# Three operands of the top-k selection are read from PSUM banks instead of SBUF

## The chip, the core and the metric

The kernel runs on one core of a Trainium2 chip. Its five engines are TensorE (PE in the profile; its weight loads are PEld), VectorE (DVE), ScalarE (ACT), GpSimd (POOL) and SyncE (SP), which here only issues DMAs. The metric is the device time of one launch in microseconds (us); lower is better. The inputs lie in the chip's memory (HBM). SBUF and PSUM are the on-chip memories; PSUM has eight banks of 128 partitions x 512 float32 numbers, and it is what matmuls write.

## What is computed

Two blocks of a language model over 256 tokens of width 1024, in float32: retention and stick-breaking attention, then a mixture of 16,384 experts chosen by product keys ("peer"), then a gating mixer, a feed-forward layer, an RWKV-7 mixer and another feed-forward layer. The change lies in the choice of the experts:

```python
q = (xb @ w_q).reshape(B, T, 8, 2, 128)                 # 8 heads, two half queries
s1 = einsum('bthd,nd->bthn', q[..., 0, :], k1)          # 128 scores each
s2 = einsum('bthd,nd->bthn', q[..., 1, :], k2)
v1, i1 = lax.top_k(s1, 16)
v2, i2 = lax.top_k(s2, 16)
cand_s = (v1[..., :, None] + v2[..., None, :]).reshape(..., 256)
cand_i = (i1[..., :, None] * 128 + i2[..., None, :]).reshape(..., 256)
top_s, pos = lax.top_k(cand_s, 16)
idx = take_along_axis(cand_i, pos)
g = softmax(top_s)
h = einsum('bthkd,btd->bthk', u_tab[idx], xb)
a = gelu(h) * g
y = einsum('bthk,bthkd->btd', a, v_tab[idx])
```

## The kernel before, in words

The kernel gathers no rows of the two expert tables. It multiplies the tokens with all 128 tiles of 128 experts (`hidden`, one tile of `u` at a time), applies gelu, multiplies by a table of gates that is zero where an expert was not chosen, and multiplies the result with all tiles of `v`. So the choice of the experts is needed only for the gates, and runs on DVE while PE works through the first tiles of `u`.

**The tiles of `u`.** Each float32 tile is split in a high and a low part, so that three matmuls of a faster format give the product. For each tile ACT makes `rows_hi` from `rows_raw` (L1349), POOL subtracts, `rows_lo = rows_raw - rows_hi` (L2301: two inputs and one output of 1024 numbers a partition in SBUF), and PE runs 8 matmuls on `rows_hi` with `x_hi` and 8 with `x_lo` (L644, L645) and then, after a wait for `rows_lo`, 8 on `rows_lo` (L648). `rows_hi` has two buffers: ACT makes that of tile t + 2 when PE has finished tile t. ACT's gelu of a tile (L1334) reads one of PSUM banks 0 to 3 and writes the table. The rows come by DMA into a ring of eight, issued by SP as PE finishes tiles. The order on each engine is that of the code. Loops of eight tiles are called rounds.

**The selection on DVE**, once for each half `c` of 128 tokens, in the order of the code: `top16` on 16 lists of 128 scores (five passes over the lists: MAX8, FIND_INDEX8, MATCH_REPLACE8, MAX8, FIND_INDEX8); the indices turned into float32 (`top_if`, L1863); the 8 x 256 sums of candidates (`cand`, L1865); `top16` on these 8 lists; shifts and masks that split a position into its two halves (L1869, L1870), the margins for the softmax (L1873, which ACT's exponential at L1358 waits for), the positions as float32 (L1874); then, for j = 0 and 1, `oh` = (position == iota) (L1879), `oh` = `oh` * index (L1884), and a sum over the last axis into `pick` (L1887). L1865, L1879 and L1884 work on 2048 numbers a partition, with operands that are broadcast from 16 at a time.

Between these steps DVE waits for its own earlier ones (`step.sync`, or `step(...)`, which marks and waits). ACT takes the exponentials of both halves in one place, after its fifth round; DVE then scales `pick` and signals `pick_ready`; PE transposes `pick` after six rounds of tiles (L664), and DVE copies the results out (L1901) and makes one-hot rows (L1912), that turn into gates from the 65th tile on. PE fills banks 4 and 5 with the transposes and banks 6 and 7 with the gates; between the expert scores (`ps`, all eight banks) and the gates nobody uses banks 6 and 7.

Of the kernel before, what the change touches and what calls it, by code (L numbers as in the profile page):

```python
# [6 lines left out]
P = 128  # L7
# [3 lines left out]
TC = SEQ // P  # L11
HEADS = 8
# [3 lines left out]
TOPK = 16  # L16
SLOTS = HEADS * TOPK
# [14 lines left out]
ALU = mybir.AluOpType  # L32
# [86 lines left out]
def build(nc, d_x, d_const, d_param, d_rows, d_ring, d_k12, d_u, d_v, d_up, d_down, d_brow, d_final, d_out, upto=99):  # L119
# [3 lines left out]
    def S(name):  # L123
        if name not in sems:
            sems[name] = nc.alloc_semaphore(name)
        return sems[name]
# [5 lines left out]
    def view(name, at, shape, dt=F32):  # L132
        return nc.alloc_sbuf_tensor_at(name, [P] + list(shape), dt, offset=base + 4 * at)
# [39 lines left out]
    def C(name):  # L173
        a, w = CONST_AT[name]
        return const[:, a:a + w]
# [12 lines left out]
    a = ARENA_AT + TC * PROJ_W  # L188
# [20 lines left out]
    a = ARENA_AT  # L209
# [5 lines left out]
    cand = view("cand", a, [TC, HEADS, TOPK, TOPK])  # L215
# [1 line left out]
    top_v = view("top_v", a, [TC, 16, TOPK])  # L217
    a += 512
    top_i = view("top_i", a, [TC, 16, TOPK], U32)
    a += 512  # L220
    top_if = view("top_if", a, [TC, 16, TOPK])
    a += 512
    best = view("best", a, [TC, HEADS, TOPK])
    a += 256
# [140 lines left out]
    PS = [nc.alloc_psum_tensor(f"bank{b}", [P, 512], F32) for b in range(8)]  # L365
# [12 lines left out]
    def wait_filled(eng, name):  # L378
        b, _, fills = plan.at[name]
        eng.wait_ge(filled[b], fills)  # L380
        return PS[b]

    def wait_drained(eng, name):
        b, k, _ = plan.at[name]
        eng.wait_ge(drained[b], k + 1)
# [15 lines left out]
    def bc(ap, shape):  # L401
        return ap.to_broadcast([P] + list(shape))

    with nc.Block() as block:  # L404
# [3 lines left out]
        def _(pe):  # L408
# [11 lines left out]
            def release_when_filled(n, name):  # L420
                b, _, fills = plan.at[name]
                release[n] = (filled[b], fills)
# [1214 lines left out]
        def _(ve):  # L1637
            V = nc.vector
            step = Steps(ve, S("dve_steps"))
# [41 lines left out]
            def copy(name, dst):  # L1681
                o = wait_filled(ve, name)
                drain(name, V.tensor_copy(dst, o[:, :]))
# [152 lines left out]
            for b in range(0, 8, 2):  # L1836
                copy(("pq", b), qT[:, 2 * b:2 * b + 2, :].rearrange("p m t -> p (m t)"))

            def top16(n, src, val, idx):

                for m in range(n):
                    step.mark(V.max(val(m)[:, 0:8], src(m)))
                step.sync()
                for m in range(n):
                    step.mark(V.max_index(idx(m)[:, 0:8], val(m)[:, 0:8], src(m)))
                step.sync()
                for m in range(n):
                    step.mark(V.match_replace(src(m), val(m)[:, 0:8], src(m), KNOCKED_OUT))
                step.sync()
                for m in range(n):  # L1850
                    step.mark(V.max(val(m)[:, 8:16], src(m)))
                step.sync()
                for m in range(n):
                    step.mark(V.max_index(idx(m)[:, 8:16], val(m)[:, 8:16], src(m)))
                step.sync()

            for c in range(TC):
                for g in range(4):
                    wait_drained(ve, ("ps", c, g))
                top16(16, lambda m: sc[:, c, m, :], lambda m: top_v[:, c, m, :], lambda m: top_i[:, c, m, :])  # L1860
                if c:
                    step.sync()
                step.mark(V.tensor_copy(top_if[:, c, :, :], top_i[:, c, :, :]))  # L1863
                v4 = top_v[:, c, :, :].rearrange("p (h j) k -> p h j k", j=2)
                step(V.tensor_tensor(cand[:, c, :, :, :], bc(v4[:, :, 0, :].unsqueeze(3), [HEADS, TOPK, TOPK]),  # L1865
                                     bc(v4[:, :, 1, :].unsqueeze(2), [HEADS, TOPK, TOPK]), ALU.add))
                flat = lambda h: cand[:, c, h, :, :].rearrange("p a b -> p (a b)")
                top16(HEADS, flat, lambda h: best[:, c, h, :], lambda h: pos[:, c, h * TOPK:(h + 1) * TOPK])
                step.mark(V.tensor_scalar(pos12[:, 0, c, :], pos[:, c, :], 4, None, ALU.logical_shift_right))  # L1869
                step(V.tensor_scalar(pos12[:, 1, c, :], pos[:, c, :], TOPK - 1, None, ALU.bitwise_and))  # L1870

                g4 = pick[:, 2, c, :].rearrange("p (h k) -> p h k", h=HEADS)
                V.tensor_tensor(g4, best[:, c, :, :], bc(best[:, c, :, 0:1], [HEADS, TOPK]), ALU.subtract).then_inc(S("margin_ready"), 1)  # L1873
                step(V.tensor_copy(pos12f[:, :, c, :], pos12[:, :, c, :]))  # L1874
                i4 = top_if[:, c, :, :].rearrange("p (h j) k -> p h j k", j=2)

                wait_filled(ve, ("ps", TC - 1, 3))
                for j in range(2):
                    step.mark(V.tensor_tensor(oh[:, j, :, :], bc(pos12f[:, j, c, :].unsqueeze(2), [SLOTS, TOPK]),  # L1879
                                              bc(C("iota")[:, 0:TOPK].unsqueeze(1), [SLOTS, TOPK]), ALU.is_equal))  # L1880
                step.sync()
                for j in range(2):
                    o4 = oh[:, j, :, :].rearrange("p (h k) a -> p h k a", h=HEADS)
                    step.mark(V.tensor_tensor(o4, o4, bc(i4[:, :, j, :].unsqueeze(2), [HEADS, TOPK, TOPK]), ALU.mult))  # L1884
                step.sync()
                for j in range(2):
                    step.mark(V.tensor_reduce(pick[:, j, c, :], oh[:, j, :, :], AX, ALU.add))  # L1887
                step.sync()
# [107 lines left out]
            for b in range(4):  # L1996
                o = wait_filled(ve, ("sp", b))
                for m in range(2):
                    n = 2 * b + m
# [191 lines left out]
            c = NRC - 1  # L2191
# [51 lines left out]
            c = NRC - 1  # L2243
# [250 lines left out]
def _program(nc, arrays, upto=99):  # L2494
    aps = [nc.dram_tensor(f"in_{n}", a.shape, F32, kind="ExternalInput").ap() for n, a in arrays.items()]
    out = nc.dram_tensor("out_0", (SEQ, D), F32, kind="ExternalOutput").ap()
    build(nc, *aps, out, upto=upto)
# [11 lines left out]
```

## Time and profile before

| | |
|---|---|
| median of 3 runs | 1954.88 us (1953.95 to 1955.27) |
| the profiled execution, its own time | 1953.33 us |
| its span, first to last instruction | 1951.5 us |
| PE busy | 1799.9 us, 92% of the span |
| POOL, DVE, ACT busy | 1094.0, 1054.9, 873.9 us |
| the selection runs | from about 355 to 487 us of the span |

The clock that TensorE was granted was 0.962 of full speed over the span, and 1.00 from 355 to 840 us. Busy time says which engine has little room; what a change is worth is read from who waits for whom in the stretch it touches.

### The profile page before, as it was taken

The page shows a single profiled execution, that of the slowest core. Times are in us where ns is not written, and L with a number is a line of the kernel's source. Part 1 is how long each engine was busy: PE and PEld are TensorE (multiplying, and loading weights), DVE is VectorE, ACT ScalarE, POOL GpSimd, SP SyncE. Part 2 cuts the span into 40 slices and gives each one's busy share as a digit, 9 for nine tenths or more (in the row PEclk, how much of TensorE's full clock was granted, in tenths as well). Part 3 has the DMA queues.
Part 4 walks back from the last instruction along what each step waited for, and adds up shares of the span by engine and source line. Part 5 has one row for each costly group of instructions (what it writes and reads, how often), then busy time and mean ns, then how long its engine had stood idle before and what let it go on. Part 6 is the DMA issues. An engine that isn't in the chain of part 4 may idle for free. (4 is left out here: it accounts for less than half of the span.)

```text
span 1951.5 us, 35793 instructions
## 1 busy us (share of the span) xinstructions
PE 1799.9 (92%) x14142; PEld 1635.3 (84%) x14142; DVE 1054.9 (54%) x1731; ACT 873.9 (45%) x1141; POOL 1094.0 (56%) x409
## 2 busy tenths in 40 slices
PE   7799778998999999999999989899969899679997
PEld 6688668988999999888888878799958689669997
DVE  5953441798447777544444443444355863555343
ACT  4247324444543333455555555455444732145443
POOL 7775537598876666555555556465537300446552
PEclk9999888999999999999999999999979899879999
DMA  7433334255554444466677625355424110224542
GB/s 286 151 130 130 116 122 172 95 165 160 174 162 141 140 140 140 156 192 193 192 235 246 214 98 181 143 194 194 150 109 169 69 24 4 110 108 173 186 178 78
DMA packets 63937, 293.71 MB, mean 151 GB/s; under 512 B 10848, under 2 KB 11232, under 8 KB 45408
## 3 DMA queue, kind: packets, MB, share of 16 engines
q1 hardware_dynamic: 63840, 292.32, 43.6%
q8 instruction: 73, 1.20, 0.3%
q14 instruction: 24, 0.20, 0.0%
HBM read 290.19 MB, written 1.05 MB: 149 GB/s over the span
## 5 line engine op out<-in xcount | busy, mean ns | idle before, releaser
L2292 POOL TENSOR_TENSOR unit_lo<-unit_raw,unit_hi 128x2048 fp32r<-128x2048 f32 x72 | 342.3, 4777 | 238.1 <-ACT unit_hi L1263 238.0
L2301 POOL TENSOR_TENSOR rows_lo<-rows_raw,rows_hi 128x1024 fp32r<-128x1024 f32 x128 | 326.6, 2556 | 130.2 <-ACT rows_hi L1367 85.2
L2309 POOL TENSOR_TENSOR a_lo<-table,a_hi 128x256 fp32r<-128x256 f32 x128 | 176.3, 1377 | 176.1 <-ACT a_hi L1391 176.1
L1957 DVE TENSOR_TENSOR rows_lo<-rows_raw,rows_hi 128x1024 fp32r<-128x1024 f32 x128 | 157.3, 1229 | 189.6 <-ACT rows_hi L1386 189.6
L644 PE MATMUL bank<-x_hi,rows_hi 128*128 128x256 f32 x1024 | 256.2, 288 | 1.7 <-ACT rows_hi L1349 1.7
L645 PE MATMUL bank<-x_lo,rows_hi 128*128 128x256 f32 x1024 | 250.7, 283 | 0.0
L1386 ACT ACTIVATE rows_hi<-rows_raw 128x1024 fp32r<-128x1024 f32 x128 | 135.7, 1060 | 171.8 <-PE bank L706 171.8
L2322 POOL TENSOR_TENSOR up_lo<-up_raw,up_hi 128x2048 fp32r<-128x2048 f32 x22 | 113.4, 5158 | 160.2 <-ACT up_hi L1440 160.2
L1263 ACT ACTIVATE unit_hi<-unit_raw 128x2048 fp32r<-128x2048 f32 x72 | 136.8, 1910 | 136.8 <-PE bank L466 92.6
L644 PEld LDWEIGHTS bank<-x_hi,rows_hi 128*128 128x128 f32 x1024 | 195.8, 191 | 1.9 <-issue 1.9
L645 PEld LDWEIGHTS bank<-x_lo,rows_hi 128*128 128x128 f32 x1024 | 196.1, 192 | 0.0
L768 PE MATMUL bank<-x_hi,up_hi 128*128 128x256 f32 x704 | 175.4, 286 | 4.6 <-DVE xf_lo L1673 4.6
L769 PE MATMUL bank<-xf_lo,up_hi 128*128 128x256 f32 x704 | 175.3, 286 | 0.0
L648 PE MATMUL bank<-x_hi,rows_lo 128*128 128x256 f32 x1024 | 145.0, 284 | 10.4 <-POOL rows_lo L2301 10.4
L648 PEld LDWEIGHTS bank<-x_hi,rows_lo 128*128 128x128 f32 x1024 | 131.8, 192 | 13.1 <-POOL rows_lo L2301 13.1
L768 PEld LDWEIGHTS bank<-x_hi,up_hi 128*128 128x128 f32 x704 | 137.1, 195 | 5.9 <-issue 5.2
L700 PE MATMUL bank<-rows_hi,a_hi 128*128 128x512 f32 x512 | 137.1, 389 | 1.8 <-ACT a_hi L1391 1.8
L769 PEld LDWEIGHTS bank<-xf_lo,up_hi 128*128 128x128 f32 x704 | 137.2, 195 | 0.7
L703 PE MATMUL bank<-rows_hi,a_lo 128*128 128x512 f32 x512 | 137.2, 389 | 0.3 <-POOL a_lo L2309 0.3
L706 PE MATMUL bank<-rows_lo,a_hi 128*128 128x512 f32 x512 | 137.0, 389 | 0.0
L1367 ACT ACTIVATE rows_hi<-rows_raw 128x1024 fp32r<-128x1024 f32 x64 | 67.7, 1059 | 154.1 <-PE bank L648 154.1
L2027 DVE SCALAR_TENSOR_TENSOR acc<-bank,param,acc 128x255 f32<-128x255 f32 x88 | 36.4, 476 | 165.9 <-ACT acc L1454 165.9
(399 smaller groups left out, 3983.9 us busy)
## 6 DMA issues: line engine op xcount, KB each, us to landing
unit_raw<-in_ring SPq DMA_DIRECT2D x77, 1024.0 KB, 4.9
rows_raw<-in_u SPq DMA_DIRECT2D x128, 512.0 KB, 3.5
rows_raw<-in_v SPq DMA_DIRECT2D x128, 512.0 KB, 3.6
up_raw<-in_up SPq DMA_DIRECT2D x44, 1024.0 KB, 6.2
down_raw<-in_down SPq DMA_DIRECT2D x22, 1024.0 KB, 5.1
const<-in_const SPq DMA_DIRECT2D x1, 1792.0 KB, 15.0
X<-in_x SPq DMA_DIRECT2D x2, 512.0 KB, 4.0
vst<-XN SPq DMA_DIRECT2D x8, 128.0 KB, 2.5
```

The costliest lines, as they stand in the source:

```text
L644: mm(o, hi[:, k, :], x_hi[:, k, :], start=k == 0, stop=False)
L645: mm(o, hi[:, k, :], x_lo[:, k, :], start=False, stop=False)
L648: m = mm(o, lo[:, k, :], x_hi[:, k, :], start=False, stop=k == KT - 1)
L700: mm(o, tokens(a_hi[q % 2], c), rows_of(rows_hi[q % 2], h), start=first, stop=False, skip_group_check=True)
L703: mm(o, tokens(a_lo[q % 2], c), rows_of(rows_hi[q % 2], h), start=False, stop=False, skip_group_check=True)
L706: m = mm(o, tokens(a_hi[q % 2], c), rows_of(rows_lo[q], h), start=False, stop=last, skip_group_check=True)
L768: mm(o, tile(up_hi, k), x_hi[:, k, :], start=k == 0, stop=False)
L769: mm(o, tile(up_hi, k), xf_lo[:, k, :], start=False, stop=False)
L1957: V.tensor_tensor(rows_lo[q][:, :], rows_raw[q][:, :], rows_hi_f[q % 2], ALU.subtract).then_inc(S("v_lo_ready"), 1)
L2292: nc.gpsimd.tensor_tensor(unit_lo[SLOT_OF[n]][:, :], unit_raw[SLOT_OF[n]][:, :], unit_hi[h % HI_SLOTS][:, :].bitcast(F32), ALU.subtract).t ...
L2301: nc.gpsimd.tensor_tensor(rows_lo[q][:, :], rows_raw[q][:, :], rows_hi_f[q % 2], ALU.subtract).then_inc(S("u_lo_ready"), 1)
L2309: nc.gpsimd.tensor_tensor(a_lo[q % 2][:, :], table[:, t, :], a_hi_f[q % 2], ALU.subtract).then_inc(S("a_lo_ready"), 1)
```

## The change

The indices as float32 are written to PSUM bank 7 (`index_bank`) instead of to `top_if` in SBUF, and L1884's multiplication reads them there. Sixteen numbers of iota are copied to bank 6 (`first_iota`), and L1879's comparison reads them there. The 8 x 16 values that are the first operand of the candidate sums are copied to bank 6 too (`first_scores`), and L1865 reads them there. Each of the three operations thus has one input in SBUF and one in PSUM where it had two in SBUF. Both copies are made again for each half. Ahead of them DVE waits until ACT has drained all eight banks of the expert scores. Nothing else is edited; PE, ACT, POOL and SP have the same instructions in the same order, and DVE has two more for each half (the copies). `top_if`'s 512 numbers a partition go, and the tensors behind it move down by as many.

```diff
-    top_if = view("top_if", a, [TC, 16, TOPK])
-    a += 512
...
+            index_bank = PS[7][:, 0:16 * TOPK].rearrange("p (m k) -> p m k", m=16)
+            first_iota = PS[6][:, 0:TOPK]
+            first_scores = PS[6][:, P:2 * P].rearrange("p (h k) -> p h k", h=HEADS)
...
-                step.mark(V.tensor_copy(top_if[:, c, :, :], top_i[:, c, :, :]))
+                for n in range(TC):
+                    for g in range(4):
+                        wait_drained(ve, ("ps", n, g))
+                step.mark(V.tensor_copy(index_bank, top_i[:, c, :, :]))
+                step.mark(V.tensor_copy(first_iota, C("iota")[:, 0:TOPK]))
                 v4 = top_v[:, c, :, :].rearrange("p (h j) k -> p h j k", j=2)
-                step(V.tensor_tensor(cand[:, c, :, :, :], bc(v4[:, :, 0, :].unsqueeze(3), [HEADS, TOPK, TOPK]),
+                step(V.tensor_copy(first_scores, v4[:, :, 0, :]))
+                step(V.tensor_tensor(cand[:, c, :, :, :], bc(first_scores.unsqueeze(3), [HEADS, TOPK, TOPK]),
                                      bc(v4[:, :, 1, :].unsqueeze(2), [HEADS, TOPK, TOPK]), ALU.add))
...
-                i4 = top_if[:, c, :, :].rearrange("p (h j) k -> p h j k", j=2)
+                i4 = index_bank.rearrange("p (h j) k -> p h j k", j=2)
...
                 for j in range(2):
                     step.mark(V.tensor_tensor(oh[:, j, :, :], bc(pos12f[:, j, c, :].unsqueeze(2), [SLOTS, TOPK]),
-                                              bc(C("iota")[:, 0:TOPK].unsqueeze(1), [SLOTS, TOPK]), ALU.is_equal))
+                                              bc(first_iota.unsqueeze(1), [SLOTS, TOPK]), ALU.is_equal))
```

## Rows read from the trace of the kernel before

**Rows 1.** Busy time by engine in three stretches of the selection, with clock.

```profile
core 0: us, PE busy (x) PEld busy (x) DVE busy (x) ACT busy (x) POOL busy (x), PEclk, DMA share, GB/s
...
380.00:394.00 14.00, 13.58 (x113) 13.58 (x114) 13.83 (x61) 6.13 (x9) 12.37 (x6) 1.00 0.54 177
394.00:412.00 18.00, 15.03 (x121) 14.42 (x121) 17.90 (x7) 6.53 (x11) 17.33 (x5) 1.00 0.45 147
...
455.00:473.00 18.00, 15.02 (x121) 14.41 (x121) 17.93 (x6) 6.52 (x11) 17.38 (x5) 1.00 0.47 146
```

**Rows 2.** Who waited for whom, 350 to 520 us: total, times, longest.

```profile
ACT rows_hi L1349 <- PE bank L648: 82.0, 45, 3.1
...
DVE keys1T L1901 <- PE bank L664: 25.1, 1, 25.1
...
PE bank L648 <- POOL rows_lo L2301: 10.2, 12, 1.2
```

**Rows 3.** Groups of instructions by shape, 350 to 512 us.

```profile
L2301 POOL TENSOR_TENSOR rows_lo<-rows_raw,rows_hi 128x1024 fp32r<-128x1024 f32 x49 | 136.5, 2795 | 38.1 <-ACT rows_hi L1349 37.8
...
L1879 DVE TENSOR_TENSOR oh<-pos12f,const 128x2048 f32<-128x2048 f32 x4 | 17.6, 4427 | 0.1
L1884 DVE TENSOR_TENSOR oh<-oh,top_if 128x2048 f32<-128x2048 f32 x4 | 17.4, 4396 | 0.1
...
L1865 DVE TENSOR_TENSOR cand<-top_v 128x2048 f32<-128x2048 f32 x2 | 4.6, 2278 | 0.0
...
L1874 DVE CAST pos12f<-pos 128x256 f32<-128x256 uint32 x2 | 0.6, 286 | 0.0
```

**Rows 4.** POOL in order of time: start, length of the row, count.

```profile
376.24 6.48 POOL L2301 TENSOR_TENSOR rows_lo<-rows_raw,rows_hi 128x1024 fp32r<-128x1024 f32 x2 [0.48 <-ACT rows_hi L1349]
...
391.45 2.40 POOL L2301 TENSOR_TENSOR rows_lo<-rows_raw,rows_hi 128x1024 fp32r<-128x1024 f32 x1 [0.47 <-ACT rows_hi L1349]
394.33 2.54 POOL L2301 TENSOR_TENSOR rows_lo<-rows_raw,rows_hi 128x1024 fp32r<-128x1024 f32 x1 [0.48 <-ACT rows_hi L1349]
397.21 22.04 POOL L2301 TENSOR_TENSOR rows_lo<-rows_raw,rows_hi 128x1024 fp32r<-128x1024 f32 x6 [0.34 <-ACT rows_hi L1349]
```

**Rows 5.** DVE in order of time, beside them.

```profile
394.64 8.78 DVE L1879 TENSOR_TENSOR oh<-pos12f,const 128x2048 f32<-128x2048 f32 x2
```

**Rows 6.** PE's matmuls on rows_lo in order of time, eight a tile.

```profile
376.83 1.12 PE L648 MATMUL bank<-x_hi,rows_lo 128*128 128x256 f32 x8
...
383.39 1.12 PE L648 MATMUL bank<-x_hi,rows_lo 128*128 128x256 f32 x8
...
397.79 1.12 PE L648 MATMUL bank<-x_hi,rows_lo 128*128 128x256 f32 x8
...
417.43 1.12 PE L648 MATMUL bank<-x_hi,rows_lo 128*128 128x256 f32 x8
...
437.59 1.12 PE L648 MATMUL bank<-x_hi,rows_lo 128*128 128x256 f32 x8
...
444.26 1.12 PE L648 MATMUL bank<-x_hi,rows_lo 128*128 128x256 f32 x8
...
458.66 1.12 PE L648 MATMUL bank<-x_hi,rows_lo 128*128 128x256 f32 x8
...
478.30 1.12 PE L648 MATMUL bank<-x_hi,rows_lo 128*128 128x256 f32 x8
```

**Rows 7.** DVE's operations with a bank among the inputs, whole program, by shape.

```profile
L1912 DVE TENSOR_TENSOR onehot<-bank,keys1T 128x512 f32<-128x512 f32 x64 | 44.3, 693 | 62.2 <-PE bank L674 62.2
```

**Rows 8.** DVE from 513 to 535 us in order of time.

```profile
513.73 0.68 DVE L1908 COPY bank<-const 128x512 f32<-128x512 f32 x1
...
516.33 18.18 DVE L1940 COPY table<-bank 128x1024 f32<-128x1024 f32 x16
```

**Rows 9.** POOL during that copying.

```profile
519.36 2.41 POOL L2301 TENSOR_TENSOR rows_lo<-rows_raw,rows_hi 128x1024 fp32r<-128x1024 f32 x1 [0.48 <-ACT rows_hi L1349]
```

**Rows 10.** DVE's last instruction ahead of pick_ready.

```profile
486.71 0.29 DVE L1894 TENSOR_TENSOR pick<-pick,stat 128x128 f32<-128x128 f32 x1
```

## The prediction

> **What bounds the kernel now.** I read first the busy time by stretch, then the waits, then the three engines in order of time. PE is the engine with the least room, and in most of the selection it has no gaps to speak of: from 380 to 394 us it is busy 13.58 of 14 us. In the two stretches in which DVE makes `oh` it is busy only 15.03 of 18 and 15.02 of 18 us, at the full granted clock of 1.00 (2.4 GHz) [rows 1]. The waits name what is missing: PE's matmuls on `rows_lo` waited for POOL 12 times, 10.2 us in all [rows 2]. No row of that view has a DMA in it for this stretch; ACT's conversions wait for PE alone (82.0 us), so they and POOL's subtractions follow PE's pace and set none of their own as long as POOL keeps up.
>
> Does POOL keep up? An undisturbed subtraction takes 2.40 us, and two of them start 2.88 us apart (391.45 and 394.33), which is PE's pace of a tile: 0.48 us are spare. But the six that begin at 397.21 take 22.04 us, 3.67 us each [rows 4], and the mean over the 49 of the selection is 2795 ns [rows 3].
>
> What slows them is read from DVE's side. L1879 and L1884 take 4427 and 4396 ns for 2048 numbers, while L1865, of the same size, takes 2278 ns [rows 3]. The extra 2.1 us is not work. POOL starts at 394.33 and ends at 396.87; DVE starts at 394.64 [rows 4, 5] and, if it works 2.28 us from POOL's end, ends its first operation at 399.1, and half of the pair's 8.78 us is 4.39, that is 399.0. So the two engines take turns: POOL waits for DVE's operation, DVE for POOL's, and each pair costs about 2.40 + 2.0 us. L1865 came first and was not held; POOL's pair beside it took 6.48 us where two take 4.80 [rows 4]. All three lines have two inputs in SBUF.
>
> **What PE loses.** The starts of L648 give it, without any modelled end. From 397.79 to 417.43 there are five tiles: 19.64 us, against 5 x 2.88 = 14.40, so 5.24 us are lost. From 458.66 to 478.30, five tiles again: 5.24 us. Around L1865, from 376.83 to 383.39, two tiles: 6.56 - 5.76 = 0.80 us; from 437.59 to 444.26, two tiles: 6.67 - 5.76 = 0.91 us [rows 6]. Together 12.19 us. This is more than the 10.2 us of waiting, since a matmul sequence that restarts after a wait does not at once run at its old pace.
>
> **The change, part by part.**
>
> L1879 and L1884, eight instructions, get one input from PSUM. Whether that ends the turn-taking is the one thing that decides. The nearest rows: L1940 reads a bank and writes 1024 numbers to SBUF 16 times in 18.18 us, without a pause from 516.33 on, and POOL's subtraction at 519.36 takes 2.41 us in the middle of it [rows 8, 9]. So DVE's writing to SBUF and reading PSUM do not hold POOL. L1912 (bank and SBUF in, SBUF out, an `is_equal` with broadcast operands) takes 693 ns for 512 numbers in all of its 64 runs [rows 7]. With one input in SBUF there is nothing left of what L1879 shares with POOL. I take the loss of 2 x 5.24 us as gone; the lower bound is that nothing is gained (the operation is held as before), the upper that all is.
>
> Their own length: L1912's fixed part is 693 - 512/0.96 = 160 ns, so 2048 numbers take 2133 + 160 = 2293 ns; L1865 gives 2278 with both inputs in SBUF. DVE saves 8 x (4.41 - 2.29) = 17.0 us. That is worth nothing by itself (slack, below).
>
> On this fixed part the Trainium skill (VectorE: DVE Perf Modes, the section on the TRN2 errata) has it the other way: it lists 58 cycles for a source in SBUF and 120 for one in PSUM. By it ten operations would cost DVE some 0.65 us more in all (an estimate from that page); by the rows above 15 ns each, 0.15 us. Neither reaches PE.
>
> L1865, two instructions, gets one input from PSUM: by the same argument 0.80 + 0.91 us. Before it stand a copy of 16 numbers and one of 128 to a bank, and the conversion of 256 indices now ends in a bank. A copy to a bank of 512 numbers took 0.68 us [rows 8], so 147 ns fixed; the three take about 0.16, 0.28 and 0.41 us. L1874, 256 numbers within SBUF, takes 286 ns [rows 3], so the conversion loses its quicker form: 0.13 us each. New on DVE: about 2 x 0.6 = 1.2 us, less than a tenth of what it saves, and none with a second SBUF input.
>
> The added wait for the drained banks stands where DVE has already done five passes over the scores; ACT's copies were over before. Cost nothing; without that cover it would be what ACT lacks, and the three operations and `margin_ready` would be queued behind it. The moved addresses cost nothing.
>
> What stays of the turn-taking: L1869 to L1874 keep SBUF inputs. POOL's subtraction beside them took 2.54 us instead of 2.40 [rows 4], inside its 0.48 us of room.
>
> **Slack and what is late next.** DVE's `pick` is ready at 487.0 [rows 10], and DVE then waits 25.1 us for PE's transposes [rows 2]; so DVE can be much later or earlier without effect. `pick_ready` hangs on ACT's exponentials, which ACT takes after its fifth round and thus by PE's pace; they move with it. With POOL at 2.40 us against 2.88, nothing is late next: PE's own 24 matmuls bound the tile.
>
> **Sum.** 1953.33 - 12.2 = 1941.1 us for an execution like the profiled one. The three runs' median is 1.55 us above that one, so the forecast for the median is 1954.88 - 12.2 = 1942.7 us. Everything behind the selection is started by semaphores, none by a time, and should move up as a whole.
>
> **Rivals.**
>
> 1. *Forecast: the whole loss goes.* 0.78. Its own range is 1941 to 1945: 1.2 us above and below for the terms, and some for the clock.
> 2. *Part goes.* The turn-taking ends for L1879 but an operand read 16 at a time from a bank runs slower, or L1884, which writes where it reads, still meets POOL. For: no row has such an operand of 2048 numbers. Against: L1912 runs at full rate with broadcasts. Half of the loss of the `oh` stretches stays: 1954.9 - 1.7 - 5.2 = 1948.0. Chance 0.08.
> 3. *The gain is given back later.* The later stages run at a lower granted clock in places (0.962 over the span), and a shift of 12 us may put them otherwise. For it nothing in the rows but that mean; the first stages behind the selection have 1.00. If half is given back: 1948.8; if all: 1954.9. Chance 0.07.
> 4. *The change does not do it: DVE holds POOL as before*, by the write of 2048 numbers. Against: L1940's writes did not. 1954.9 and a little. Chance 0.04.
> 5. *Slower: reading a bank makes `pick` late.* The ten operations take 4 x 4.43 + 4 x 4.40 + 2 x 2.28 = 39.9 us now, 3.99 us each. Were each of them L us long, `pick` would be ready 10 x (L - 3.99) us later than before, and PE, which now comes 25.1 us after it, would end its transposes by 10 x (L - 3.99) - 25.1 us later than before. This passes zero at L = 6.5 us and tells from no change at 6.9 us; at 7.0 us the time is 1954.9 + 5.0 = 1959.9 us. For it only that no row has such an operand (16 numbers at a time from a bank, 2048 in all); against it the 693 ns of L1912, which scale to 2.29 us. Chance 0.03.
>
> The Trainium skill (SBUF — State Buffer, the section on who interferes with whom) says that a DVE instruction with two SBUF inputs contends with a GpSimd instruction that reads SBUF, and that one with at most one, outside the two-port modes, does not. By that rule case 4 is excluded; the trace agrees as far as it goes (2.41 us beside L1940, 3.67 us beside L1879).
>
> **Numbers.** Point 1942.7. The range must take in the first case with its bounds and reach some way to the partial ones: 1939.5 to 1947.5. A measurement of this kernel tells about 0.2%, 3.9 us, from no change. Faster by more than that: cases 1 and 2 and half of 3, 0.91. Within: 0.06. Slower: 0.03.
>
> **What would show each step.** In the profile after: L2301 at 2.40 to 2.45 us throughout the selection, its 49 at a mean near 2410 ns; the wait of L648 for POOL from 10.2 us to below 1; L1879, L1884 and L1865 at 2.28 to 2.30 us; the starts of L648 2.88 us apart everywhere; DVE busy less by about 16, POOL by about 19 us; DVE's wait at L1901 still 24 to 26 us. Wrong would be: POOL at 3.7 us still (case 4); DVE at 2.3 us but POOL not at 2.4 (the write holds it); the stretch shorter by 12 us and the span not (case 3).

## The result, and the profile after

The changed kernel takes 1942.18 us, median of 6 runs (1938.46 to 1944.43), and the kernel before, run beside it, 1953.96 us (1949.76 to 1955.27). The ratio is 0.9938, with a 95% interval of 0.9925 to 0.9952. That is 11.8 us less, where 12.2 had been forecast; the forecast for the median itself was 1942.7. The profiled execution took 1941.93 us, its span is 1940.0 us.

The page of the changed kernel, busy time by engine, to be held against the table of before:

```profile
PE 1798.1 (93%) x14142; PEld 1635.1 (84%) x14142; DVE 1041.6 (54%) x1735; ACT 873.7 (45%) x1141; POOL 1075.5 (55%) x409
```

PE does what it did, in 11.5 us less. POOL is busy 18.5 us less with the same 409 instructions, DVE 13.3 us less with four more. Who waited for whom in the changed kernel, 350 to 508 us (total, times, longest), answers to [rows 2]; the code's lines have moved, so L646 is the former L648, L1347 the former L1349 and L1908 the former L1901:

```profile
ACT rows_hi L1347 <- PE bank L646: 69.8, 45, 2.8
...
DVE keys1T L1908 <- PE bank L662: 25.1, 1, 25.1
...
PE bank L646 <- POOL rows_lo L2308: 0.5, 2, 0.3
```

PE's waits for POOL fell from 10.2 us to 0.5. DVE's own wait for PE's transposes is still 25.1 us. Of the 13.3 us of work that DVE was spared it waits 1.0 us longer for ACT's exponentials (8.8 us where it was 7.8); the other 12.3 are the time by which PE, and all that follows its pace, comes sooner.

The groups of the changed kernel by shape, 350 to 500 us, answer to [rows 3]:

```profile
L2308 POOL TENSOR_TENSOR rows_lo<-rows_raw,rows_hi 128x1024 fp32r<-128x1024 f32 x49 | 117.8, 2406 | 44.5 <-ACT rows_hi L1347 44.5
...
L1891 DVE TENSOR_TENSOR oh<-oh,bank 128x2048 f32<-128x2048 f32 x4 | 9.0, 2284 | 0.1
L1886 DVE TENSOR_TENSOR oh<-pos12f,bank 128x2048 f32<-128x2048 f32 x4 | 9.0, 2284 | 0.1
...
L1872 DVE TENSOR_TENSOR cand<-bank,top_v 128x2048 f32<-128x2048 f32 x2 | 4.6, 2292 | 0.1
...
L1881 DVE CAST pos12f<-pos 128x256 f32<-128x256 uint32 x2 | 2.8, 1387 | 0.0
L1880 DVE TENSOR_TENSOR pick<-best 128x128 f32<-128x128 f32 x2 | 2.7, 1368 | 0.1
...
L1868 DVE CAST bank<-top_i 128x256 f32<-128x256 uint32 x2 | 0.9, 428 | 0.1
...
L1871 DVE COPY bank<-top_v 128x128 f32<-128x128 f32 x2 | 0.6, 283 | 0.0
```

The subtraction's mean went from 2795 to 2406 ns, and the comparison and the multiplication from 4.4 to 2.28 us each. The candidate sums, at 2292 ns, are no faster than before; they only stopped holding POOL. Two small operations, L1880 and L1881, have become much longer on average (1368 and 1387 ns); the order in time shows why. DVE in the changed kernel:

```profile
393.11 2.44 DVE L1880 TENSOR_TENSOR pick<-best 128x128 f32<-128x128 f32 x1
395.48 0.28 DVE L1881 CAST pos12f<-pos 128x256 f32<-128x256 uint32 x1
395.80 4.49 DVE L1886 TENSOR_TENSOR oh<-pos12f,bank 128x2048 f32<-128x2048 f32 x2
400.31 4.49 DVE L1891 TENSOR_TENSOR oh<-oh,bank 128x2048 f32<-128x2048 f32 x2
...
499.41 0.29 DVE L1908 COPY keys1T<-bank 128x128 f32<-128x128 f32 x1 [25.11 <-PE bank L662]
```

And POOL beside it:

```profile
393.01 2.40 POOL L2308 TENSOR_TENSOR rows_lo<-rows_raw,rows_hi 128x1024 fp32r<-128x1024 f32 x1 [0.47 <-ACT rows_hi L1347]
395.89 2.41 POOL L2308 TENSOR_TENSOR rows_lo<-rows_raw,rows_hi 128x1024 fp32r<-128x1024 f32 x1 [0.48 <-ACT rows_hi L1347]
398.77 2.40 POOL L2308 TENSOR_TENSOR rows_lo<-rows_raw,rows_hi 128x1024 fp32r<-128x1024 f32 x1 [0.47 <-ACT rows_hi L1347]
```

L1880 is 128 numbers, with two inputs in SBUF. It starts 0.10 us behind POOL's subtraction and ends when that has ended: it was held. In the other half it slipped in at 0.29 us, and the conversion behind it, which has one input, was held instead (2.49 us). POOL pays next to nothing for either (2.40 and 2.44 us). The large operations with an input in a bank run right through the next subtractions, which start 2.88 us apart and last 2.40 us, against 3.67 us each in [rows 4].

**One measure for all runs.** The whole clock of a run moves by some us for reasons outside the selection (last section), so I read each profile also by the distance from the start of PE's first matmuls on `rows_lo` to DVE's first copy of the transposed `pick`: before 362.33 to 512.14 = 149.81 us, after 361.82 to 499.41 = 137.59 us. The difference is 12.22 us, against 12.19 in the prediction's sum. "Stretch" below is this distance. It ends at 500 to 515 us of the span and says nothing of what an edit does to the time behind that; experiment 3 shows that this matters.

### The profile page after: what moved, and what is told of

It reads as the page before. It is cut to its first block and busy times, and to the rows that moved or that the text cites. A ratio compares the mean times of both kernels' runs of the same rounds, so it can differ in the third digit from the quotient of the medians.

```text
span 1940.0 us, 35805 instructions
## 1 busy us (share of the span) xinstructions
PE 1798.1 (93%) x14142; PEld 1635.1 (84%) x14142; DVE 1041.6 (54%) x1735; ACT 873.7 (45%) x1141; POOL 1075.5 (55%) x409
## 5 line engine op out<-in xcount | busy, mean ns | idle before, releaser
L2308 POOL TENSOR_TENSOR rows_lo<-rows_raw,rows_hi 128x1024 fp32r<-128x1024 f32 x128 | 307.8, 2406 | 136.8 <-ACT rows_hi L1365 85.3
L646 PE MATMUL bank<-x_hi,rows_lo 128*128 128x256 f32 x1024 | 144.0, 283 | 0.7 <-POOL rows_lo L2308 0.7
L646 PEld LDWEIGHTS bank<-x_hi,rows_lo 128*128 128x128 f32 x1024 | 132.0, 192 | 1.3 <-POOL rows_lo L2308 1.3
L458 PE MATMUL bank<-unit_hi,x_hi 128*128 128x512 f32 x272 | 110.4, 406 | 16.5 <-DVE proj L1681 8.3
```

Of the source, the lines that this page charges most:

```text
L646: m = mm(o, lo[:, k, :], x_hi[:, k, :], start=False, stop=k == KT - 1)
L2308: nc.gpsimd.tensor_tensor(rows_lo[q][:, :], rows_raw[q][:, :], rows_hi_f[q % 2], ALU.subtract).then_inc(S("u_lo_ready"), 1)
```

## The experiments

Theory T: DVE and POOL take turns when a DVE instruction reads two inputs from SBUF beside a subtraction of POOL; the later one waits for the earlier one to end; POOL's delay beyond its 0.48 us of room is PE's. The rivals are named in each expectation.

**1 and 2. One edit alone.** The first keeps only this of the change (and the wait for the drained banks):

```diff
+                step.mark(V.tensor_copy(first_iota, C("iota")[:, 0:TOPK]))
...
-                                              bc(C("iota")[:, 0:TOPK].unsqueeze(1), [SLOTS, TOPK]), ALU.is_equal))
+                                              bc(first_iota.unsqueeze(1), [SLOTS, TOPK]), ALU.is_equal))
```

> Only the comparison (L1879) gets its iota from a bank; indices and candidate values stay in SBUF. Theory T (two inputs in SBUF make DVE and POOL take turns, whichever engine's instruction comes second waits for the first to end): the comparison takes 2.28 us, the multiplication still 4.4 us; of the 5.24 us that PE loses per half about 3.1 go and about 2.15 stay (a first held subtraction costs PE 0.65, each one right behind it 1.5), and the 1.7 us of the candidate sums stay. PE loses about 6.0 us in the selection, the time is about 1948 us against 1954. Rival W (DVE's write of 2048 numbers holds POOL, and all three edits are needed together): no change, 1954 us. Rival A (the moved addresses did it; here nothing is moved): no change, 1954 us.

The second keeps only this:

```diff
-                step.mark(V.tensor_copy(top_if[:, c, :, :], top_i[:, c, :, :]))
+                step.mark(V.tensor_copy(index_bank, top_i[:, c, :, :]))
...
-                i4 = top_if[:, c, :, :].rearrange("p (h j) k -> p h j k", j=2)
+                i4 = index_bank.rearrange("p (h j) k -> p h j k", j=2)
```

> Only the multiplication (L1884) gets its index from a bank. T: the mirror image of the first experiment: comparison 4.4 us, multiplication 2.28 us, POOL's subtraction held only beside the comparison, PE loses about 6.0 us in the selection, about 1948 us. W or A: 1954 us. If the multiplication, which writes where it reads, still met POOL, it would stay at 4.4 us.

Measured: 1945.02 us (ratio 0.996, 0.9945 to 0.9975) and 1947.42 us (0.9981, 0.9972 to 0.999), the kernel before beside them 1952.26 us. Groups by shape of the first, 350 to 520 us:

```profile
L1890 DVE TENSOR_TENSOR oh<-oh,top_if 128x2048 f32<-128x2048 f32 x4 | 14.0, 3544 | 0.1
L1885 DVE TENSOR_TENSOR oh<-pos12f,bank 128x2048 f32<-128x2048 f32 x4 | 9.0, 2284 | 0.1
```

And of the second:

```profile
L1884 DVE TENSOR_TENSOR oh<-pos12f,const 128x2048 f32<-128x2048 f32 x4 | 17.6, 4428 | 0.1
L1889 DVE TENSOR_TENSOR oh<-oh,bank 128x2048 f32<-128x2048 f32 x4 | 9.0, 2285 | 0.1
L1870 DVE TENSOR_TENSOR cand<-top_v 128x2048 f32<-128x2048 f32 x2 | 6.3, 3159 | 0.0
```

In each only the line that was edited is free. In the second kernel the candidate sums started while a subtraction was running and were held too (3159 ns, where they took 2278). The stretches are 143.62 and 143.47 us, 6.19 and 6.34 less than before. T had 6.2, that is 12.2 less the 6.0 that PE still loses. That the multiplication writes where it reads makes no difference. (In the first kernel the multiplication's mean is 3544 and not 4400 ns: in the first half it begins at 400.99, near the end of the subtraction that runs from 399.04 to 401.46, and is held 0.3 us only; the one behind it takes 4.4. PE loses as much either way.) Rivals W and A are out: each edit works alone, and with nothing moved in SBUF.

**3. The candidate sums alone.**

```diff
+                step(V.tensor_copy(first_scores, v4[:, :, 0, :]))
-                step(V.tensor_tensor(cand[:, c, :, :, :], bc(v4[:, :, 0, :].unsqueeze(3), [HEADS, TOPK, TOPK]),
+                step(V.tensor_tensor(cand[:, c, :, :, :], bc(first_scores.unsqueeze(3), [HEADS, TOPK, TOPK]),
```

> Only the candidate sums (L1865) get an input from a bank. T: POOL's subtraction beside them goes from about 4.1 to 2.4 us, the 0.80 and 0.91 us that PE lost there are gone, all else as before: 1954 - 1.7 = 1952.3 us, which the profile can show and the timing hardly. W or A: nothing changes at the candidate sums.

Measured: 1953.78 us against 1952.26 (1.001, 1.0001 to 1.0018). The stretch is 148.29 us, 1.52 less than before. POOL ahead of and beside the sums, which DVE makes from 377.83 to 380.12 us:

```profile
375.05 2.40 POOL L2307 TENSOR_TENSOR rows_lo<-rows_raw,rows_hi 128x1024 fp32r<-128x1024 f32 x1 [0.48 <-ACT rows_hi L1349]
377.93 2.42 POOL L2307 TENSOR_TENSOR rows_lo<-rows_raw,rows_hi 128x1024 fp32r<-128x1024 f32 x1 [0.48 <-ACT rows_hi L1349]
```

At the candidate sums PE loses nothing any more: its matmuls on `rows_lo` start 2.88 us apart there. 0.2 of the 1.7 us comes back in the second half, where the first held tile costs PE 3.74 us instead of 3.53.

The timing doesn't show the gain; its interval even lies on the other side by 0.01 to 0.18%. The median is 1.5 us above that of before. A reason stands 290 us behind the stretch, where PE passes from the tiles of `u` to those of `v` after a wait of 1.81 us for ACT. Its first matmuls there, in the kernel before:

```profile
803.30 1.20 PE L703 MATMUL bank<-rows_hi,a_lo 128*128 128x512 f32 x4 [0.29 <-POOL a_lo L2309]
804.33 1.08 PE L706 MATMUL bank<-rows_lo,a_hi 128*128 128x512 f32 x4
```

And in this one:

```profile
803.46 2.07 PE L703 MATMUL bank<-rows_hi,a_lo 128*128 128x512 f32 x4
805.33 1.52 PE L706 MATMUL bank<-rows_lo,a_hi 128*128 128x512 f32 x4
```

The granted clock over the four microseconds from 803.30 is 0.63 of full speed, where the kernel before has 1.00 at this place. From the first matmuls on `v` to those two tiles later it is 7.44 us instead of 6.13, so 1.31 us are lost. In the profiles 1.5 us is won and 1.3 given back, and the launch gains next to nothing by this edit. I count this part as shown for the selection and not for the whole.

All five profiles of kernels whose candidate sums read a bank show this (the changed kernel 7.49 and 7.48, experiments 5 and 9 7.73 and 7.67, this one 7.44 us), and none of the other six (6.11 to 6.13). Whether the edit brings it about or the moment at which PE gets there is open: four of the five are also the four that get there first (788 to 791 us), and only experiment 3, at 802.0 us beside the 801.8 of the kernel before, speaks against the moment.

**4. The copies, read by nobody.** All three copies to the banks are made, beside the conversion to SBUF; the three operations read SBUF.

```diff
                 step.mark(V.tensor_copy(top_if[:, c, :, :], top_i[:, c, :, :]))
+                step.mark(V.tensor_copy(index_bank, top_i[:, c, :, :]))
+                step.mark(V.tensor_copy(first_iota, C("iota")[:, 0:TOPK]))
...
+                step(V.tensor_copy(first_scores, v4[:, :, 0, :]))
```

> The copies of iota and of the candidate values and the second conversion of the indices to the banks are made, and read by nobody: all three operations keep two SBUF inputs. T: as before, 1954 us; DVE's copies (about 0.9 us a half) are hidden, PE loses 12.2 us as before. A rival by which the time came from DVE's order, its waits or the use of banks 6 and 7 expects 1942 us.

Measured: 1953.63 us (1.0004, 0.9995 to 1.0014); stretch 149.54 us, 0.27 less than before. Groups by shape, 350 to 520 us:

```profile
L2311 POOL TENSOR_TENSOR rows_lo<-rows_raw,rows_hi 128x1024 fp32r<-128x1024 f32 x52 | 143.3, 2765 | 39.0 <-ACT rows_hi L1349 38.5
L1894 DVE TENSOR_TENSOR oh<-oh,top_if 128x2048 f32<-128x2048 f32 x4 | 17.4, 4395 | 0.1
L1889 DVE TENSOR_TENSOR oh<-pos12f,const 128x2048 f32<-128x2048 f32 x4 | 15.5, 3906 | 0.1
L1875 DVE TENSOR_TENSOR cand<-top_v 128x2048 f32<-128x2048 f32 x2 | 8.5, 4238 | 0.1
```

The rival that expected 1942 us is out: the copies, the waits and the use of banks 6 and 7 are worth nothing by themselves and cost nothing that can be measured. The candidate sums come 0.5 us later than in the kernel before; now POOL is first and they are held, 4238 ns where they took 2278.

**5 and 9. The other operand.** In the changed kernel the position comes from a bank and iota from SBUF:

```diff
-                step(V.tensor_copy(pos12f[:, :, c, :], pos12[:, :, c, :]))
+                step(V.tensor_copy(places, pos12[:, :, c, :]))
...
-                    step.mark(V.tensor_tensor(oh[:, j, :, :], bc(pos12f[:, j, c, :].unsqueeze(2), [SLOTS, TOPK]),
-                                              bc(first_iota.unsqueeze(1), [SLOTS, TOPK]), ALU.is_equal))
+                    step.mark(V.tensor_tensor(oh[:, j, :, :], bc(places[:, j, :].unsqueeze(2), [SLOTS, TOPK]),
+                                              bc(C("iota")[:, 0:TOPK].unsqueeze(1), [SLOTS, TOPK]), ALU.is_equal))
```

> The changed kernel, but in the comparison it is the position that is read from a bank and iota that is read from SBUF. T (what counts is that at most one input is in SBUF): as the changed kernel, comparison 2.28 us, subtractions 2.40 us, 1942 us. Rival I (the second input as written always comes by the way that POOL shares, and must be the one in PSUM): the comparison is held again, 4.4 us, PE loses about 4.3 us more, 1946.5 us.

Measured: 1938.43 us (0.9932, 0.9915 to 0.9949), stretch 137.59 us, to the hundredth that of the changed kernel. Groups by shape, 350 to 520 us:

```profile
L1885 DVE TENSOR_TENSOR oh<-bank,const 128x2048 f32<-128x2048 f32 x4 | 9.0, 2285 | 0.1
...
L1880 DVE CAST bank<-pos 128x256 f32<-128x256 uint32 x2 | 0.8, 418 | 0.0
```

Rival I is out: either input may be the one in PSUM. The conversion to a bank is not held here (418 ns), while that within SBUF was, in the changed kernel (2.49 us). This goes beyond T, which speaks of two inputs: the conversion has one. For it the place of the output does matter. Within SBUF it takes its short form (0.29 us when free) and can be held. With its output in a bank it takes 0.41 to 0.43 us and was never held: that of the changed kernel at 374.28 took 0.43 us in the middle of a subtraction (372.85 to 375.25). It isn't that every operation with one input is held: the sum over `oh` (L1894, the former L1887), which reads 2048 numbers of SBUF while subtractions run, takes 2281 ns on average before and after. As the median lay below that of the changed kernel, both were run once more, side by side:

> The changed kernel once more, on the same chip and beside the next one. T: PE loses none of the 12.2 us in the selection; about 12 us less than the kernel before in the same job.

> The kernel of the fifth experiment once more (position from a bank, iota from SBUF). The stretches of both had the same length, so T expects the same time as the changed kernel beside it, within 0.2%; that the fifth experiment's median lay 3.7 us below the changed kernel's would then be the granted clock of the runs (0.967 against 0.962 over the span), which takes either value in both kernels. A rival, that the position's conversion to a bank saves PE something, expects 3 to 4 us less in this job too.

Measured: 1943.23 us (0.9956, 0.9943 to 0.9968) and 1940.35 us (0.9952, 0.9938 to 0.9965) against 1952.07 us. Both stretches are 137.59 us. The changed kernel is 8.8 us below before this time and was 11.8 below the first time. The ratios of the two can't be told apart, but the medians lie 2.9 us apart, which is near what the rival wanted (3 to 4 us), so the clock must decide. At a granted clock of 0.960 to 0.963 the median of the changed kernel is 1943.4 us (four runs) and that of the other 1944.4 us (two); at 0.966 to 0.968 they are 1940.4 (two) and 1939.6 us (four). At the same clock there is no gain of 3 us. What isn't shown is that the higher clock comes to both kernels equally often: it came to 4 of 12 runs of the changed kernel and to 7 of 10 of this one.

**6. Reads or the write.** The kernel before, but the comparison writes to banks 4 to 7:

```diff
+                    step(V.tensor_tensor(four_banks.rearrange("p (s a) -> p s a", a=TOPK), bc(pos12f[:, j, c, :].unsqueeze(2), [SLOTS, TOPK]),
+                                         bc(C("iota")[:, 0:TOPK].unsqueeze(1), [SLOTS, TOPK]), ALU.is_equal))
...
+                    step(V.tensor_tensor(o4, four_banks.rearrange("p (h k a) -> p h k a", h=HEADS, k=TOPK), bc(i4[:, :, j, :].unsqueeze(2), [HEADS, TOPK, TOPK]), ALU.mult))
```

> The kernel before, but the comparison, with both inputs in SBUF, writes its 2048 numbers to banks 4 to 7, and the multiplication reads them there and writes to SBUF; one j after the other. T (reads decide): the comparison is held, about 4.4 us, and holds POOL, each time as a first held subtraction (0.65 to 0.9 us for PE), the multiplication is free at 2.3 us. PE loses 4 x 0.8 + 1.7 for the candidate sums = about 5 us in the selection: 1947 us. W (the write to SBUF decides): the comparison is free, the multiplication is held: also about 1947 us by time, so the lengths in the profile tell: W wants the comparison at 2.3 and the multiplication at 4.4 us.

Measured: 1947.1 us (0.9972, 0.9961 to 0.9984); stretch 142.84 us, 6.97 less than before. DVE in order of time:

```profile
395.98 4.38 DVE L1885 TENSOR_TENSOR banks<-pos12f,const 128x2048 f32<-128x2048 f32 x1
400.40 2.29 DVE L1888 TENSOR_TENSOR oh<-banks,top_if 128x2048 f32<-128x2048 f32 x1
402.72 4.42 DVE L1885 TENSOR_TENSOR banks<-pos12f,const 128x2048 f32<-128x2048 f32 x1
407.18 2.29 DVE L1888 TENSOR_TENSOR oh<-banks,top_if 128x2048 f32<-128x2048 f32 x1
```

PE's matmuls on `rows_lo` beside them:

```profile
399.13 1.12 PE L649 MATMUL banks<-x_hi,rows_lo 128*128 128x256 f32 x8
402.67 1.22 PE L649 MATMUL banks<-x_hi,rows_lo 128*128 128x256 f32 x8 [0.49 <-POOL rows_lo L2305]
405.65 1.12 PE L649 MATMUL banks<-x_hi,rows_lo 128*128 128x256 f32 x8
409.44 1.21 PE L649 MATMUL banks<-x_hi,rows_lo 128*128 128x256 f32 x8 [0.76 <-POOL rows_lo L2305]
```

The operation that writes nothing to SBUF is held (4.40 us), and the one that writes all 2048 numbers there, with one input from a bank, is free (2.29 us). So on DVE's side it is the two reads. What of POOL's side they meet, its reads or its write, no run separates, for the subtraction is the same in all. A held subtraction with free ones between costs PE 0.76 to 1.01 us each time (3.54 or 3.79 against 2.88, and 0.10 in the tile behind), where one right behind another costs 1.5.

**7. Smaller pieces in SBUF.**

```diff
+                    for s in range(0, SLOTS, SLOTS // 4):
+                        w = slice(s, s + SLOTS // 4)
+                        step.mark(V.tensor_tensor(oh[:, j, w, :], bc(pos12f[:, j, c, w].unsqueeze(2), [SLOTS // 4, TOPK]),
+                                                  bc(C("iota")[:, 0:TOPK].unsqueeze(1), [SLOTS // 4, TOPK]), ALU.is_equal))
```

> The kernel before with the comparison and the multiplication each cut in four pieces of 512 numbers, all inputs in SBUF. T (turns, and an instruction never shares): each of the 32 pieces waits for a subtraction to end, so takes up to 2.4 + 0.69 = 3.1 us where its work is 0.69; 32 x 3.1 = 99 us against 35 us now, pick is 64 us later, 25 of them slack: about 1954 + 39 = 1993 us. POOL's subtraction takes at most 2.4 + 0.7 = 3.1 us. Rival F (the two share the bandwidth, each slowed in proportion): DVE's sum is that of before plus 24 fixed parts of 0.15 us, 3.6 us more, all hidden: 1954 us.

Measured: 1955.78 us (1.0016, 1.0006 to 1.0026), stretch 150.75 us, 0.94 more than before. T's number was far off, and F's came near for the wrong reason. The two lines' durations (min/median/max):

```profile
L1881 DVE TENSOR_TENSOR oh<-pos12f,const x16: 678/2815/2892, 396.4 to 489.1; 128x512 f32<-128x512 f32 x16
```

```profile
L1888 DVE TENSOR_TENSOR oh<-oh,top_if x16: 677/2888/2902, 416.7 to 505.0; 128x512 f32<-128x512 f32 x16
```

A piece is either free, at 0.68 to 0.69 us, or it waits out a subtraction and takes 2.78 to 2.90; none of the 32 lies between, so nothing is slowed in proportion, as F has it. The 32 pieces need 67.9 us in all and not 99: I had reckoned with 3.1 us for every piece and left out that POOL idles 0.48 us in each tile, so that POOL's pace stays 2.88 us, and now and then two pieces pass in one gap. DVE's `pick` is then about 33 us later, which is past the 25.1 us of slack, and the waits (350 to 520 us) say so:

```profile
PE bank L644 <- ACT rows_hi L1349: 5.5, 2, 3.8
...
PE bank L664 <- DVE pick L1898: 4.9, 1, 4.9
...
ACT pick L1358 <- DVE pick L1873: 3.8, 1, 3.8
...
PE bank L648 <- POOL rows_lo L2305: 1.4, 3, 0.6
```

PE's wait for POOL is down to 1.4 us from 10.2, with all inputs in SBUF, and what was gained is lost to a late margin (ACT waits 3.8 us, PE for ACT 3.8) and a late `pick` (4.9).

## Why the prediction was right, point by point

*What bounds the stretch.* PE's pace, broken by POOL's held subtractions: right. With these gone nothing was late next; in the stretch of the changed kernel PE's tiles are 2.88 us apart but for the places that the kernel before has too (the first tile, and those at ACT's exponentials).

*Turn-taking, read from a pair of durations.* Right. Experiments 1, 2, 5 and 6 show it from four sides: an operation with two inputs is held only when both are in SBUF, either may be moved away, and its write has no part. Experiment 4 shows that nothing else in the change has a part. What the prediction didn't see is the conversion with one input, held in the kernel before (L1863, 868 ns on average) and in the changed one (2.49 us).

*The size, 12.19 us.* Right for the selection: the stretch shortened by 12.22. Experiments 1 (6.19 of 6.2), 2 (6.34), 3 (1.52 of 1.7) and 6 (6.97 of about 7.2) come out of the same per-tile losses.

*"Everything behind the selection ... should move up as a whole."* This step held but for one place. The span shortened by 11.5 us: 0.5 was won ahead of the stretch, and 1.2 lost behind it. The loss is that of experiment 3, 1.36 us at the passage to `v` (6.13 against 7.49 us), less 0.1 won elsewhere, and it is there in the second profile of the changed kernel too (7.48 us). The sum had no term for it, and the error was small against the range. The point for the median (1942.7, measured 1942.18) came out closer than the sum deserves: the kernel before, measured beside it, was itself 0.9 us below the 1954.88 that the sum started from. That part was luck.

*DVE's prices.* The operations at 2284 and 2292 ns (forecast 2293), the copies at 167 and 283 (160 and 280), the conversion at 428 (410). What the Trainium skill (VectorE: DVE Perf Modes, the section on the TRN2 errata) charges for a PSUM source, 62 cycles more, did not show: 2284 to 2292 ns against 2278 with both inputs in SBUF, 6 to 14 ns.

*One term was mis-sized, without effect on the time.* "DVE busy less by about 16": it was 13.3. I had costed what "stays of the turn-taking" for POOL (0.14 us) and not for DVE: L1880 and L1881 were held for some 2.2 us each once, 4.3 us in all. I had also priced the index conversion of before at L1874's 286 ns; it took 868, so that moving it to a bank (428 ns) saved 0.9 us where I had booked a cost of 0.26. This is hidden behind DVE's 25.1 us of waiting.

*The rivals.* The second (part goes) and fourth (no effect) are excluded by the durations. The third (given back later, at a lower granted clock in places) happened in small: 1.36 of 12.2 us, at one place, where it had half or all. How much arrives in a whole launch is less sure than the profiles suggest, 11.8 us the first time and 8.8 the second; in the second, comparing only runs of like clock, it is 9.6 us (0.961 to 0.963) and 9.3 us (0.966 to 0.969). That is less than the 10.9 us which 12.2 less 1.36 leaves, and no run shows where the rest went. The fifth, a `pick` that comes too late, did not happen here, but experiment 7 shows it to be real: there DVE spent the slack and 8 us more.

*The chances.* By the prediction's own list, cases 1 and 2 and half of 3 make 0.895, not 0.91, and what is left for "within" is 0.075, not 0.06.

## What to carry to other kernels

When an operation takes about twice as long as another of the same size and engine, look what the neighbour engine does in that time: here the excess was neither work nor bandwidth but waiting in turn, and the cost lay not with the slow DVE instruction (it had 25 us of slack) but with the POOL instruction that it held, which PE needed. A small broadcast operand (16 to 256 numbers) that is moved to an idle PSUM bank takes a large DVE operation off the shared way at the price of one short copy. Cutting the operation in pieces protects POOL too, but makes DVE pay a whole subtraction for most pieces. And a gain that is read from the distance between two events in the profile is to be followed to the end of the program: the candidate sums did what they should in the selection, and most of what they won was lost again 290 us later.

## What the runs showed of the hardware that I had not expected

A DVE instruction of 0.29 us with two SBUF inputs can last 2.44 us, for it waits out the whole subtraction that began 0.10 us ahead of it; POOL doesn't notice. And which of two small operations is hit changes with 0.1 us of timing: in the profile of the kernel before the same lines took 292 and 286 ns in both halves.

Much of the spread between runs comes from one place. The six runs of the changed kernel are 1941.93, 1942.44, 1943.10 and 1944.43 us with a granted clock of 0.961 to 0.963 over the span, and 1938.46 and 1939.63 us with 0.967 and 0.968. Two profiles, one of either kind (the changed kernel, then experiment 5), whose stretches in the selection are equal, end 5.4 us apart. Read from the starts of the same DVE instructions, they are 1.0 us apart at the stretch, 1.6 us from 1680 to 1705 us, and 5.4 us from 1756 us on. The 3.8 us between arise in these hundred microseconds:

```profile
core 0: us, PE busy (x) PEld busy (x) DVE busy (x) ACT busy (x) POOL busy (x), PEclk, DMA share, GB/s
...
1687.00:1787.00 100.00, 81.94 (x476) 72.83 (x477) 56.97 (x84) 45.82 (x54) 52.88 (x11) 0.84 0.41 153
```

```profile
1686.00:1786.00 100.00, 82.40 (x508) 73.70 (x509) 59.70 (x88) 48.07 (x57) 54.56 (x11) 0.91 0.43 163
```

In the one PE spends more of that time at 1.2 GHz instead of 2.4 (mean 0.84 against 0.91 of full speed), and has issued 476 matmuls where the other has issued 508. What decides it was not tried. Ahead of the selection the profiles differ as well: the stretch begins between 360.8 and 364.1 us in kernels that are the same up to there. An edit worth 1 to 2 us can't be seen in the timing beside this, and has to be read from distances within the profile.
